# The mask product of an attention kernel moved behind its bank's score products, with 64 columns of weights

## The reference

```python
key_chunk = jnp.arange(S) // CHUNK                      # CHUNK = 64, S = 2048
q_chunk = (bi * Q_BLOCK + jnp.arange(Q_BLOCK)) // CHUNK # Q_BLOCK = 128
mask = key_chunk[None, :] <= q_chunk[:, None]
s = jnp.einsum('bqhmd,bshmd->bhmqs', qi, k) * scale     # 8 heads, m = 0, 1, d = 64
s = jnp.where(mask, s, -jnp.inf)
p = jax.nn.softmax(s, axis=-1)
pd = p[:, :, 0] - lam * p[:, :, 1]
o = jnp.einsum('bhqs,bshe->bqhe', pd, v)
```

## Time and profile before

| | us |
|---|---|
| median of 3 runs | 3097.42 (3095.65 to 3098.68) |
| profiled execution, its own time | 3094.02 |
| span of the profile | 3092.2 |
| PE busy / weight loads busy | 2932.8 / 2527.8 |
| DVE / ACT / POOL busy | 1494.0 / 1234.0 / 841.1 |
| mean granted clock of TensorE | 0.985 of full speed |

### The profile page before, as it was taken

How to read it: one execution, slowest core, us unless ns; L and a number is a source line. 1 busy time by engine, 2 the same in 40 slices (tenths; PEclk the granted TensorE clock), 3 DMA queues, 4 the chain that set the end, 5 groups by cost and what they waited for, 6 DMA issues and landing times. The chain is left out here.

```text
span 3092.2 us, 43110 instructions
## 1 busy us (share of the span) xinstructions
PE 2932.8 (95%) x15680; PEld 2527.8 (82%) x15680; DVE 1494.0 (48%) x2352; ACT 1234.0 (40%) x2779; POOL 841.1 (27%) x944
## 2 busy tenths in 40 slices
PE   7899999999999999866997999999999999999999
PEld 7888889888888888755886888888888888888887
DVE  5577776767676777765332322222223222222223
ACT  5566666666666666554222222211111222211111
POOL 4524333242424243222001222212122222212121
PEclk9999999999999999897998999999999999999999
DMA  7633424242424233101245211111115311111112
GB/s 247 239 123 102 137 88 151 88 151 90 151 95 142 101 108 111 53 16 53 102 163 188 84 55 54 51 44 41 41 41 217 109 55 54 49 46 39 42 41 75
DMA packets 167593, 296.80 MB, mean 96 GB/s; under 512 B 10512, under 2 KB 117008, under 8 KB 151056
## 3 DMA queue, kind: packets, MB, share of 16 engines
q1 hardware_dynamic: 160944, 269.65, 26.3%
q10 hardware_dynamic: 6496, 25.17, 2.1%
HBM read 244.45 MB, written 50.33 MB: 95 GB/s over the span
## 5 line engine op out<-in xcount | busy, mean ns | idle before, releaser
L1502 PE MATMUL banks<-u,w_hi 128*128 128x512 f32 x2048 | 632.1, 390 | 10.4 <-POOL w_lo L1387 10.4
L290 PE MATMUL proj<-w_hi,u_ring 128*128 128x384 f32 x2048 | 591.6, 349 | 7.1 <-ACT qkv L301 3.8
L1502 PEld LDWEIGHTS banks<-u,w_hi 128*128 128x128 f32 x2048 | 385.3, 188 | 90.9 <-POOL w_lo L1387 10.8
L1445 ACT ACTIVATE relu<-banks 128x512 f32<-128x512 f32 x128 | 76.6, 598 | 955.3 <-PE banks L1502 955.3
L1397 POOL TENSOR_TENSOR hid_lo<-relu_sq,hid_hi 128x512 fp32r<-128x512 f32 x128 | 165.7, 1295 | 1022.3 <-ACT hid_hi L1448 1022.3
L1485 DVE TENSOR_TENSOR y<-banks,y 128x512 f32<-128x512 f32 x256 | 176.8, 691 | 460.6 <-PE banks L1519 460.6
L1502 PE MATMUL banks<-u,w_lo 128*128 128x512 f32 x1024 | 399.1, 390 | 0.0
L1519 PE MATMUL banks<-w_hi,hid_hi 128*128 128x512 f32 x1024 | 398.3, 389 | 0.0
L1519 PE MATMUL banks<-w_lo,hid_hi 128*128 128x512 f32 x1024 | 398.3, 389 | 0.0
L1519 PE MATMUL banks<-w_hi,hid_lo 128*128 128x512 f32 x1024 | 398.3, 389 | 0.0
L290 PEld LDWEIGHTS proj<-w_hi,u_ring 128*128 128x128 f32 x2048 | 377.3, 189 | 10.0 <-ACT qkv L301 5.7
(11 more groups left out here) (108 smaller groups left out, 4966.7 us busy)
## 6 DMA issues: line engine op xcount, KB each, us to landing
u_ring<-u_scratch SPq DMA_DIRECT2D x112, 1024.0 KB, 5.1
w_raw<-in_mlp_w SPq DMA_DIRECT2D x128, 512.0 KB, 4.2
u_scratch<-u_ring SPq DMA_DIRECT2D x16, 1024.0 KB, 4.1
w_raw<-in_a_w_in SPq DMA_DIRECT2D x96, 128.0 KB, 4.5
p_all<-in_x SPq DMA_DIRECT2D x16, 512.0 KB, 4.2
rows_scratch<-o_sum SPq DMA_DIRECT2D x128, 64.0 KB, 1.6
o_in<-rows_scratch SPq DMA_DIRECT2D x16, 512.0 KB, 4.9
x_res<-in_x SPq DMA_DIRECT2D x16, 512.0 KB, 5.6
```

The source lines that it names most:

```text
L290: last = pe.matmul(proj[:, 0:3 * HD], u[:, part, kt, :], w[:, kt, :], start=(kt == 0 and part == 0 and w is w_hi), stop=(kt == KT - 1 and ...
L1502: last = pe.matmul(banks[:, e, :], w[:, j % 2, kt, :], u[:, n * TPB:(n + 1) * TPB, kt, :], start=(kt == 0 and w is w1_hi and u is u_hi), s ...
```

## The change

Behind the change the mask product is the third of its bank instead of the first. `q_hi` now opens the accumulation of the bank, the mask product closes it, and where a piece ends with the masked bank it is the mask product that counts `scored` up. The weights are `mask_l[:, 0:64]`, 64 columns in place of 128, and the product writes 64 partitions of PSUM in place of 128; it streams 64 columns as before. No wait is added or removed.

```diff
-                    if masked:
-                        pe.matmul(scores[:, at, width - DH:width], mask_l[:, :], mask_r[:, :],
-                                  start=True, stop=False, skip_group_check=True)
-                    pe.matmul(scores[:, at, 0:width], q_hi[:, m, rows], k_s[h % 2][:, m, keys],
-                              start=not masked, stop=False, skip_group_check=True)
-                    last = pe.matmul(scores[:, at, 0:width], q_lo[:, m, rows], k_s[h % 2][:, m, keys],
-                                     start=False, stop=True, skip_group_check=True)
+                    pe.matmul(scores[:, at, 0:width], q_hi[:, m, rows], k_s[h % 2][:, m, keys],
+                              start=True, stop=False, skip_group_check=True)
+                    last = pe.matmul(scores[:, at, 0:width], q_lo[:, m, rows], k_s[h % 2][:, m, keys],
+                                     start=False, stop=not masked, skip_group_check=True)
+                    if masked:
+                        last = pe.matmul(scores[0:DH, at, width - DH:width], mask_l[:, 0:DH], mask_r[:, :],
+                                         start=False, stop=True, skip_group_check=True)
```

## The result

The changed kernel takes 3124.4 us, median of 6 runs (3122.04 to 3129.24), against 3098.25 us before, timed beside it (3095.65 to 3104.69). The ratio is 1.0084 with a 95% interval of 1.0071 to 1.0097: 26 us slower. The profiled execution has a span of 3120.2 us, 28.0 more than before.

The account below looks back on a forecast made before the run. PE was taken to bound the attention stage. Width 0.055 plus shape 0.015 gave 0.07 us on each of 256 mask products, 18 us, 17 to 18 after waits; from 3097.4 the forecast was 3115 us, range 3092 to 3160.

Parts of the forecast that it names:

- The bound: Attention stage: PE is what the others wait for, so a microsecond on its stream moves the end by nearly one.
- The price of the mask product before: On PE: 0.12 us each, 0.11 of it the uncovered load behind; 31 us for 256.
- (1) The place: Mask product behind its bank's score products: one load stays uncovered, only another line's; costed at nothing, 0.3 us in all.
- (2) The semaphore: `scored` counted up by the mask product where it ends the piece: the moment all three are through doesn't move; nothing.
- (3) The width: Mask's weight load, 64 columns for 128: loses the fast path and lies uncovered, 0.055 us each.
- Rival B: No difference: mask load taken early under `q_lo`, or PE's added time fills existing waits; -3 us, 3094; chance 0.19.
- (4) The shape: Weights of 128 by 64 among 128 by 128 on PE: changing shape costs 0.015 us for each mask product.
- My upper bound of 0.33: Shape term's top: array runs empty on both sides of the mask product, 0.16 us more ahead and 0.17 behind.
- rival A: Array runs empty at each change of shape: 0.16 to 0.39 us each, 41 to 100 us, 3138 to 3197; chance 0.22.
- Rival C: Faster: mask uses half the array, the load behind goes ahead under `q_lo`; 22 us less, 3076; chance 0.09.

Follow-up runs that it names:

- e6: The change made only in query blocks 2 to 9 of each head (128 of 256 mask products), the others as before: 3122.21 us, ratio 1.0072.
- e1: The changed kernel's place for the mask product, but with 128 columns of weights and the full array: 3094.71 us, ratio 0.9987 to the kernel before.
- e10: Changed kernel with 128 columns, but in blocks 0 to 7 both mask products of a step stand behind its scores: 3099.35 us, ratio 1.0001.
- e2: The changed kernel with 66 columns of weights (two zero) and 66 output partitions in place of 64: 3095.81 us, ratio 0.9985 to the kernel before.
- e9: The kernel before, but in blocks 0 to 7 both mask products of a step stand ahead of its scores, 128 columns: 3093.26 us, ratio 0.9982.
- e4: The changed kernel with each mask product split in two of 32 keys, both with 64 columns of weights: 3128.22 us, ratio 1.0097 to the kernel before.
- e8: The kernel before with each mask product issued twice in a row, both with 128 columns: 3102.1 us, ratio 1.0012.

## Why the prediction came out as it did

**Direction and range** were right: slower, 3124 in 3092 to 3160. The size, 26 us against the forecast's 17.6, is half as much again, and that it is no farther off is luck: the price on the stream was more than three times too small (0.07 us against 0.23), and the share of it that waits take up was far too small as well (almost nothing against half), and the two errors work against each other.

**The bound.** That PE is what the others wait for in the attention is right mainly for blocks 2 to 9, where 23 of the 26 us are (e6). "Some 3% of PE's time in the stage is waiting" was read from a list that shows a wait only as far as it exceeds the overhang of the record ahead, up to 0.16 us each time; the list also was taken as a mean over the stage, while its waits lie in blocks 0, 1 and 8 to 15. In block 10 the wait of 0.39 stood there with 0.23. By the table, half of the stream's additional time is absorbed (26 of 51 to 59 us).

**The price of the mask product before**, 0.12 us of which 0.11 is the load behind it, holds: without it, blocks 4 to 7 lose 0.13 for each, and a twin behind it adds 0.04.

**(1) The place, at nothing:** nearly. It gives 4 us, which I had as a loss of 0.3; that a transpose behind a mask product is delayed by 0.035 and not 0.083 us was not in the rows that I read.

**(2) The semaphore, at nothing:** fits, for this change: e1 has it too and is not slower. In e10 it comes much later, and the last head is longer.

**(3) The width, 0.055 us for the uncovered narrow load:** the load is uncovered in the changed kernel, as I had it (720.41, behind the stream), but it takes 0.03 us and not 0.055: the pace of the float32r loads around it was the wrong measure. The reason that I gave for its being uncovered was wrong, too. I took the high end since the present load isn't taken early; but e2 shows a load of 66 columns under `q_lo`, at no cost, so what holds the load of 64 back is the change of shape. Rival B had this right as a mechanism: with the full shape its 3 us less would have been the result (e2).

**(4) The shape, 0.015 us:** the term that was mis-sized most. The engine stands for 0.09 us at each of the two changes, and the mask's own stream of 0.03 lies open besides, 0.2 us together; e2 shows that nothing of it remains when the shape stays. I took the nearest row, the change of type, and that row was about something else. Even its 0.01 us isn't the change of type: e2 has the same change of type without it. My upper bound of 0.33 was itself 0.03 too low, as it left out that the next load starts together with the mask product today, so that the mask's stream would come on top of the 0.17.

The Trainium skill's sentence that a change of the tiling mode drains the engine ("TensorEngine Tiling (Array Packing)", "Key Properties") fits the trace if 64 columns are such a mode, as a drain that is shorter than the recorded ends say: 0.09 of 0.16 us ahead, and 0.09 of 0.17 behind. So rival A, to which I gave 0.22, had the mechanism as far as the rows tell it, and the forecast did not. Its price per product, 0.16 to 0.39 us, held 0.23, and its total of 41 to 100 us failed by the same hidden waits. The sign that I had named for it, a mask product over 0.16 us behind the stream, doesn't appear (0.09), and neither does the forecast's, a next load 0.03 us behind the mask product (0.15).

**Rival C**, a load ahead of the mask product under the same score product: in no kernel here.

## What to carry to other kernels

A matmul with 64 columns of weights among full ones pays on both sides, 0.09 us each and 0.23 in all here, far more than the narrower load can give; with two idle columns more (66 in place of 64) the price is gone and the narrow load is free. Price an edit on the matrix engine by distances from start to start, and do it for each block of a loop: a list of waits doesn't show those shorter than the overhang of a matmul's record, and these decide how much of the price arrives. Small products that break the order of loads are best put side by side, so that they leave one load uncovered together, as long as nothing that others wait for comes later by it: ahead of the scores the pair gained 5 us (e9), behind them nothing (e10).

## What the runs showed of the hardware that was not expected

A load of 128 bf16 columns behind a float32r product waits until that product has streamed (0.27 us idle ahead of it in e1's row); a load of 66 bf16 columns at the same place starts with the product, 0.17 us earlier, though its own record is longer (112 against 98 ns, means of the 256 in e2 and e1). Behind a `q_lo` product of 128 columns it starts 0.05 us after the product. Behind either, the float32r load stays uncovered with its 0.10 to 0.12 us.

Fewer columns were not the shorter load: from start to start, 64 bf16 columns took 0.03 us (e4), 128 bf16 columns 0.01 us (e8) and 128 float32r columns 0.11 us.

The last head, where PE has no projections to do, has a clock of its own: the granted clock there was 0.86 of full speed in the profiled execution before and 0.78 in e10's, while all heads before it ran at 1.00 in both.
